# Fourteen of sixteen up projection groups as seven half-block products, and up and down units in alternation, in a one-core decoder layer

## The reference

```python
def channel_mlp(x, g, w_up, w_down):
    h = rmsnorm(x, g)
    u = jnp.maximum(jnp.einsum('btd,df->btf', h, w_up), 0)
    return jnp.einsum('btf,fd->btd', u * u, w_down)
```

## Time and profile before

| | |
|---|---|
| time, median of 3 runs | 2390.11 us (2389.84 to 2390.34) |
| span of the profiled execution | 2388.1 us (that execution's own time is not given apart from its span; the median lies 2.0 us above the span) |
| PE busy | 2362.5 us, 99% of the span |
| DVE busy | 1377.4 us, 58% |
| ACT busy | 963.6 us, 40% |
| DMA | 224.28 MB, 94 GB/s |

### The profile page before, as it was taken

How to read it: one execution, slowest core, us unless ns; L and a number is a source line. 1 busy time by engine, 2 the same in 40 slices (tenths; PEclk the granted TensorE clock), 3 DMA queues, 4 the chain that set the end, 5 groups by cost and what they waited for, 6 DMA issues and landing times.

```text
span 2388.1 us, 33521 instructions
## 1 busy us (share of the span) xinstructions
PE 2362.5 (99%) x13086; PEld 2016.6 (84%) x13086; DVE 1377.4 (58%) x3162; ACT 963.6 (40%) x2050; POOL 79.3 (3%) x136
## 2 busy tenths in 40 slices
PE   9999999999999999999999999999999999999998
PEld 8988888888897888888998788888888879889996
DVE  4478554456378654455456854554656785555555
ACT  4445433334345533334333543333434454333332
POOL 3000000000000000000000210000010000000000
PEclk9999999999999999999999999999999999999999
DMA  6212323333511223324421233223444122222221
GB/s 193 79 45 90 96 97 98 96 109 106 170 55 54 81 96 97 96 90 132 147 80 37 68 99 97 90 96 97 133 124 133 45 67 88 77 84 80 88 80 66
DMA packets 175402, 224.28 MB, mean 94 GB/s; under 512 B 15107, under 2 KB 126308, under 8 KB 175228
## 3 DMA queue, kind: packets, MB, share of 16 engines
q1 hardware_dynamic: 162636, 192.63, 25.8%
q10 hardware_dynamic: 6448, 19.40, 2.3%
q0 software_dynamic: 6160, 10.11, 1.6%
HBM read 210.72 MB, written 12.60 MB: 94 GB/s over the span
## 4 chain that ended last, share of the span: by engine, by line
PE 95%; DVE 4%; ACT 1%; issue 1%; DVEq 0%; ACTq 0%
PE ps L2066 28%; PE ps L2068 28%; PE ps L2067 27%; PE ps L2077 2%; PE ps L2207 2%; PE ps L2187 1%; PE ps L2196 1%; PE ps L2253 1%; PE ps L2256 1%; DVE w_lo L1177 1%; PE ps L2103 0%; PE ps L2596 0%; PE ps L2115 0%; PE ps L2232 0%; DVE w_lo L1173 0%
## 5 line engine op out<-in xcount | busy, mean ns | idle before, releaser
L2068 PE MATMUL ps<-a_hi,w_lo 128*128 128x512 f32 (+2 forms) x1672 | 583.9, 349 | 0.0
L2066 PE MATMUL ps<-a_hi,w_hi 128*128 128x512 f32 (+2 forms) x1672 | 582.1, 348 | 0.6 <-DVE a_lo L1181 0.2
L2067 PE MATMUL ps<-a_lo,w_hi 128*128 128x512 f32 (+2 forms) x1672 | 582.0, 348 | 0.0
L702 ACT ACTIVATE w_hi<-w_raw,gains 128x256 fp32r<-128x256 f32 (+1 forms) x576 | 253.2, 521 | 411.3 <-PE ps L2068 290.6
L2066 PE MATMUL ps<-w_hi,u_all 128*128 128x512 f32 x1024 | 403.8, 394 | 0.0
L2068 PE MATMUL ps<-w_hi,u_all 128*128 128x512 f32 x1024 | 403.8, 394 | 0.0
L2067 PE MATMUL ps<-w_lo,u_all 128*128 128x512 f32 x1024 | 401.3, 392 | 0.0
L2066 PEld LDWEIGHTS ps<-a_hi,w_hi 128*128 128x128 f32 x1672 | 315.8, 189 | 43.1 <-DVE a_lo L1181 1.4
L2067 PEld LDWEIGHTS ps<-a_lo,w_hi 128*128 128x128 f32 x1672 | 314.0, 188 | 40.9
L2068 PEld LDWEIGHTS ps<-a_hi,w_lo 128*128 128x128 f32 x1672 | 314.2, 188 | 39.4
L1181 DVE TENSOR_TENSOR x<-x,ps 128x512 f32<-128x512 f32 (+1 forms) x288 | 196.5, 686 | 259.8 <-PE ps L2068 241.9
(11 more groups left out here) (378 smaller groups left out, 2336.1 us busy)
## 6 DMA issues: line engine op xcount, KB each, us to landing
w_raw<-in_w_up_dram SPq DMA_DIRECT2D x128, 512.0 KB, 3.7
w_raw<-in_w_down_dram SPq DMA_DIRECT2D x128, 512.0 KB, 3.5
w_raw<-in_w_out_dram SPq DMA_DIRECT2D x32, 512.0 KB, 3.5
w_raw<-in_w_in_dram SPq DMA_DIRECT2D x24, 580.0 KB, 4.9
w_raw<-in_w_in_dram SPq DMA_DIRECT2D x22, 512.0 KB, 3.7
w_raw<-in_w_in_dram SPq DMA_DIRECT2D x32, 256.0 KB, 2.9
wide<-in_x_prompt_dram ACTq DMA_DIRECT2D x12, 512.0 KB, 4.6
x<-in_x_prompt_dram ACTq DMA_DIRECT2D x9, 512.0 KB, 6.2
```

Source lines behind the costliest of these rows:

```text
L702: ins = eng.activation(w_hi[b][:, k * n:(k + 1) * n][:, s], src[:, s], ACT.Copy, scale=gain[:, a:a + 1])
L2066: eng.matmul(out, lh, rh, start=(k == ks[0]), stop=False)
L2067: eng.matmul(out, lh, rl, start=False, stop=False)
L2068: ins = eng.matmul(out, ll, rh, start=False, stop=(k == last))
```

## The change

For 14 of the 16 up units of a quarter (all but U(0, 0) and U(0, 1)), the product of a 256 x 1024 block of weights with a 1024 x 512 block of tokens is seen as 2 x 2 blocks, and made with seven half-block products in place of eight, after the scheme of Strassen in Winograd's form. A half-block product is 4 steps of contraction x 3 = 12 matmuls of 256 tokens (320 in products 0, 1, 2 and 6 of the fourth quarter). Around it:

- The norm's gain goes onto the tokens: DVE takes each turned half tile out of PSUM times the gain into `x_all` (`take_tile`, two operations for a tile), and ACT and DVE split from there. Weights of up units are no longer scaled.
- Four sums of token blocks, and their split, are made once in a quarter (`x_sums`, `t_high_part`, `t_low_part`).
- For each such unit DVE makes four sums of weight blocks (`sum_forms`), ACT seven rounded parts (`high_form`), DVE seven rests (`low_form`), each of 512 elements; they lie in a ring of nine slots in what were the two unit buffers.
- The seven results are added up by ACT (`take_copy`) and DVE (`take_sum`, seven steps) into `c_at` in the tile `wide`; ACT then does relu, square and copy in SBUF (`square_up`), DVE the rest (`low_up`).
- Up and down units alternate: U(c, 0), D(c-1, 0), U(c, 1), D(c-1, 1), so that U(7, 1) is unit 42, where it was unit 41.
- Memory: the bias moves into a region that the MLP overwrites and is fetched again by POOL in each quarter; two of the tiles ahead lie in `PT`; the squares of `stats_ahead` are written to a region that holds token sums until all products are done, so it waits for `m_done`.
- In DVE's `step`, the pieces for the next quarter now stand at the end, behind the loop over the down unit's results.

```diff
+MLP_ORDER = [("U", 0, 0), ("U", 0, 1)]
+for _c in range(1, NC):
+    MLP_ORDER += [(kind, _c - (kind == "D"), half) for half in range(2) for kind in "UD"]
+MLP_ORDER += [("D", NC - 1, 0), ("D", NC - 1, 1)]
...
+FORMS_OF = "A11 A12 S1 S2 S4 S3 A22".split()
...
             def stats_ahead(q, b):
 
+                eng.wait_ge(m_done.sem, m_done.at(q, 0))
...
-                    if u == UNITS - 4 and not last:
-                        scale_ahead(q + 1, 0)
-                    if u == UNITS - 3 and not last:
-                        take_ahead(q + 1, 0)
-                    if u == UNITS - 2 and not last:
-                        scale_ahead(q + 1, 1)
-                    if u == UNITS - 1 and not last:
-                        take_ahead(q + 1, 1)
...
+                        eng.wait_ge(dn_read.sem, dn_read.at(q, 2 * NT * c))
+                        next_part(0)
+                        if before is not None:
+                            low_sum(before, 0)
+                        next_part(1)
                         for n, (j, R) in enumerate(down_tiles(last, u)):
...
+                            if n < 3:
+                                next_part(n + 2)
...
+                        next_part(5)
+                    if u == UNITS - 4 and not last:
+                        scale_ahead(q + 1, 0)
+                    if u == UNITS - 3 and not last:
+                        take_ahead(q + 1, 0)
+                    if u == UNITS - 2 and not last:
+                        scale_ahead(q + 1, 1)
+                    if u == UNITS - 1 and not last:
+                        take_ahead(q + 1, 1)
...
+                def product(u, f, w, right):
+
+                    eng.wait_ge(f_split.sem, f_split.at(q, 7 * seven(u) + f + 1))
+                    hi, lo = form_at(w_hi_all, u, f), form_at(w_lo_all, u, f)
+                    out = product_bank(seven(u), f)[:, 0:w]
+                    for k in range(4):
+                        rh, rl = right(k, w)
+                        eng.matmul(out, hi[:, k, :], rh, start=(k == 0), stop=False)
+                        eng.matmul(out, hi[:, k, :], rl, start=False, stop=False)
+                        ins = eng.matmul(out, lo[:, k, :], rh, start=False, stop=(k == 3))
+                    ins.then_inc(m_done.sem, 1)
...
                 def step(u, kind, c, half):
                     if u == UNITS - 3 and not last:
-                        eng.wait_ge(up_read.sem, up_read.at(q + 1, 0))
+                        eng.wait_ge(cp_ok.sem, cp_ok.at(q + 1, 0))
+                        eng.wait_ge(c_add.sem, c_add.at(q + 1, 0))
                         turn_ahead(q + 1, 0)
```

More of the change, by code:

```diff
@@ L56 @@
 WMAX = KT * TMW
+FORM = 512
+T_ALL = 6424
+T_SECOND = 4376
+RING = 9
+N_PLAIN = 2
 def unit_of(u):
@@ L193, in hymba_layer @@
         bgate = sb("bgate", [P, 2 * HM])
+        kk_forms = other("kk_forms", [P, 2, P + TMAX], F32R)
         kk = sb("kk", [P, 2, P + TMAX])
@@ L229, in hymba_layer @@
         oms = sb("oms", [NS, HM, DV], where=phase)
+        bias = sb("bias", [P, H, 2 * P], where=phase)
         phase.close()
@@ L368, in unit_shape @@
             kind, i, w = unit_of(u)
[L369 to L380, removed]
+            return (4, 512) if kind == "O" or kind == "M" and mlp_unit(u)[0] == "D" else (KT, w)
         block = ctx.enter_context(nc.Block())
@@ new lines, in hymba_layer, with staging, x_flat @@
+        HT = TQ // 2
+        def staging(last):
+            T, ws = (TMAX, HT + NS) if last else (TQ, HT)
+            line = flat(wide)
+            c_at = [line[:, i * T:(i + 1) * T] for i in range(2)]
+            at = 2 * T + ws
+            s1, r6, h5, s5 = (line[:, a:b] for a, b in ((2 * T, at), (at, at + HT), (at + HT, at + 2 * HT), (at + 2 * HT, at + 2 * HT + NS)))
+            return ws, c_at, s1, r6, h5, s5
+        def x_flat(last):
+            w = TMAX + NS if last else TMAX
+            starts = (4 * w, 8 * w + (2 * TQ if last else 4 * TMAX))
+            return [x_all[:, at:at + 4 * v].rearrange("p (k t) -> p k t", k=4) for at, v in zip(starts, (w, TMAX))]
@@ L481, in turned_bank, with t_src, product_bank, ahead_tile @@
+        def t_src(last, name):
+            one, two = x_flat(last)
+            end = TMAX if last else TQ
+            return {"T1": one[:, :, HT:end], "T3": one[:, :, 0:HT], "T2": two[:, :, 0:HT], "T4": two[:, :, HT:end]}[name]
+        def product_bank(at, n):
+            return ps[(7 * at + n + 2) % 4]
+        def ahead_tile(j):
+            return PT[:, 2 * j:2 * j + 2, :].rearrange("p a b -> p (a b)") if j < 2 else xn_tile(j)
+        def spare():
+            return t_plain[:, 0:D]
         def turned_bank(q, n):
@@ new lines, in plain_up @@
+                def plain_up(u):
+                    kind, c, half = mlp_unit(u)
+                    for n, (t, s) in enumerate(up_order(u, NN)):
+                        off, w = splits[s]
+                        o = half * 2 * NN + n
+                        eng.wait_ge(up_out.sem, up_out.at(q, o + 1))
+                        if n == 0 and half:
+                            eng.wait_ge(u_split.sem, u_split.at(q, 2 * NN))
+                        elif n == 0 and last:
+                            eng.wait_ge(turned.sem, turned.at(q, 2 * NT))
+                        mine = c_at[t][:, off:off + w]
+                        eng.activation(mine, ps[(o + 2) % 4][:, 0:w], ACT.Relu).then_inc(up_read.sem, 1)
+                        eng.wait_ge(up_read.sem, up_read.at(q, o + 1))
+                        eng.activation(mine, mine, ACT.Square).then_inc(u_sq.sem, 1)
+                        eng.wait_ge(u_sq.sem, u_sq.at(q, o + 1))
+                        eng.activation(u_hi[0][:, half * 2 + t, off:off + w], mine, ACT.Copy).then_inc(u_high.sem, 1)
@@ L1988, in step @@
-                            eng.wait_ge(u_sq.sem, u_sq.at(q, o + 1))
-                            low(l, o, t, off, w)
-                            if n == NN - 1 and not end and u != U_M:
-                                split_vec(eng, nq, nu, 1, i)
+                            low_up(u, t, off, w, half * 2 * NN + n + 1)
+                        if half:
+                            for n in (3, 4, 5):
+                                next_part(n)
+                        else:
+                            t_low_part(2)
```

694 lines of the change are left out of this document (505 added, 189 removed).

## The result

| kernel | median us (lowest to highest) | profiled execution's span |
|---|---|---|
| before | 2390.23 (2389.84 to 2390.92, 4 runs) | 2388.1 |
| changed | 2403.95 (2402.36 to 2404.09, 4 runs) | 2402.2 |

The changed kernel takes 1.0056 times as long (95% interval 1.0042 to 1.007). It is slower by 0.56%, where 2382 us and a faster kernel were forecast, and it lies 1 us above the range.

A forecast was written before the change was run, and what follows sets the result against it. PE, busy 99% of the span, was taken as the bound, so time is matmuls plus PE's new waits. 64.6 us saved less 56.3 of waits gave 8.3 us, a 2382 us median; range 2358 to 2403 us (8 in 10).

The forecast's parts named there:

- What a changed unit saves: Up units on PE: 11.12 to 10.01 us in three quarters, 12.56 to 11.26 in the fourth; together 64.6 us saved.
- the second rival: 256-column matmuls on PE run at 0.1133 us instead of 0.1192; all at that pace gives 2358 us; chance 0.22.
- DVE in the steady run: Alternating MLP units: DVE's 10.5 us list fits a down unit's 11.12 us, so new vector and scalar work costs nothing.
- The thin cover: Rival in the changed units: products wait 0.2 us each, 2393 us, or 0.4 us, 2404 us; chance 0.08.
- 1, ahead of the MLP: Before the MLP, four times: PE waits for later takes, copies and rests of tiles, 2.5 us each, total 10.0.
- 2, first changed unit: First seven-product unit, four times: products 2 and 5 come late by 0.3 and 0.9 us, total 4.8.
- 3, U(7, 1) to D(6, 1): Between these units, three times: PE's transposes wait for last addition, squares and scaling, 5.7 us each, total 17.1.
- 4, ahead of D(7, 1): Before this down unit, three times: second `scale_ahead` waits for D(7, 0)'s last result, 2.95 us each, total 8.9.
- 5, next quarter: Start of next quarter, three times: `take_ahead` begins only when the last result is read, 5.15 us each, total 15.5.
- the sum: Whole program: 64.6 us saved less 56.3 of PE waits is 8.3 us, median 2382 us; given 0.40.
- The cold start: PE restarts at half pace behind its waits, 2.5 us each: 2397 us for six waits, 2404 with D(7, 1)'s; chance 0.28.
- the first rival: PE starts cold again behind its waits at quarter ends, 2.5 us each, making the kernel slower, 2397 or 2404 us; chance 0.28.

The follow-up runs named there:

- Experiment 5: Tiles moved in SBUF; in the changed kernel the weight ring shifted 64 bytes: 2392.98 us, 128 bytes: 2394.51, 32 bytes: 2405.90; weights and activations together 64 bytes: 2404.25 us.
- experiment 3: The kernel before with its last `take_ahead` (next quarter's second tile) moved behind the loop of the last down unit: 2411.98 us, 21.8 us more.
- e7_before_pad: The kernel before with 64 bytes left free between the weights and the activations in SBUF: 2393.43 us in one run, 2.5 us more.

## Why the prediction was wrong

**What a changed unit saves: right.** 84 x 0.1192 = 10.01 us was forecast and 9.97 measured, 11.26 and 11.29 in quarter 4. 42 x 1.15 + 14 x 1.27 = 66.1 us against the 64.6 of the forecast. The faster pace that the second rival asked for did not come by itself; it took a shift of 64 bytes, and then for four of seven products.

**DVE in the steady run: right.** No wait of PE there. The thin cover did not show.

**The five places: each there, the sizes close.** In us, over the whole program; places 1 and 2 from the timelines of both kernels, the clock from the starts of matmuls:

| place | forecast | measured | clock behind it |
|---|---|---|---|
| 1, ahead of the MLP | 10.0 | 13.5 (3.1, 3.1, 3.3 and 4.0) | 1.6, in quarter 4 |
| 2, first changed unit | 4.8 | 4.6 (11.50 - 9.97 = 1.53 in three quarters, none in the fourth) | none |
| 3, U(7, 1) to D(6, 1) | 17.1 | 17.3 | 7.2 |
| 4, ahead of D(7, 1) | 8.9 | 8.0 | 6.2 |
| 5, next quarter | 15.5 | 14.7 | 7 |

The waits make 58.1 us against 56.3. That error and the one in the saving all but cancel.

**The step that failed is the sum, which priced the waits by their length alone.** The cold start was worked out as a rival, 2.5 us each, and given 0.28. It was set aside because "the waits are short, and weight loads or transposes may fall into them". The windows show 0.46 us of PE's work and 0.03 of weight loads in 5 us: all that PE had left to do stood behind the wait, in program order, and that could be read from the order beforehand. The rival's own number with place 4, 2404 us, is what was measured: 9 x 2.5 = 22.5 us against 20.4 us at these nine waits, and 1.6 at a tenth. Its size was in part luck: 2.5 us came from the program's start, where the granted clock read 1.00, and the single prices are 1.7 to 3.0. What the first rival took from the Trainium skill ("TensorE: Matmul & The Clock Gate", HAM oscillation) is what these rows show, at waits of 2.67 us too. The sum as it should have stood: 2382 - 1.5 + 1.8 + 22 = 2404 us against 2403.95.

**The chances.** The argument against the rival was a guess, the one for it came from rows 9, so it should have had the larger chance. The range ended at 2403, 1 us below the rival's own 2404, for no reason that the text gives.

**The range's other end**, the faster pace, rested on a row that had been read rightly (the alternation is real) without its cause. Experiment 5 gives its size here: some 10 us, by a move that the change did not make.

## What to carry to other kernels

When PE is the bound and a change gives it new waits, price each as its length plus a restart at half clock, unless the order shows work of PE in the wait. Here that was 1.4 to 2.8 us behind every wait of 4.9 us or more, and 1.5 to 3.0 us behind about half of those of 2 to 2.7 us. The row to look at is the granted clock in a window over the wait, not the list of waits. An operation moved from ahead of a loop to behind it can cost more than the arithmetic saved: one such move in the kernel before cost 22 us, and putting two of them back in the changed one gave 33. Where no work can be found for the wait, multiplications whose result nobody reads kept the clock up and gave 16 us. And where waits of 2 us stand, a difference of some us between two kernels can be the clock: count the stretches at half clock in both traces before it is put down to the edit.

## What the runs showed of the hardware

- Whether a short wait loses the clock differs from one execution to the next. In the traces of the ten kernels with seven products and of experiment 3, counted over all waits of PE of one length (the price is what the matmuls behind it took longer than at full clock):

| wait of PE, us | place | lost the clock | price, us |
|---|---|---|---|
| 5.65 to 6.05 | 3 | 18 of 18 | 1.4 to 2.8 |
| 4.9 | 5 | 18 of 18 | 1.5 to 2.7 |
| 2.67 | 4 | 11 of 18 | 1.5 to 3.0 |
| 2.0 to 2.1 | 1 | 21 of 40 | 1.5 to 1.7 |

A window behind place 4 of the changed kernel, where the clock fell, and one over its wait at place 1 in quarter 1, where it did not:

```profile
572.00:576.00 4.00, 4.00 (x20) 3.87 (x21) 1.60 (x2) 3.11 (x13) 0.00 (x0) 0.62 0.30 78
```

```profile
232.50:234.50 2.00, 0.05 (x1) 0.00 (x0) 1.88 (x3) 1.98 (x3) 0.00 (x0) 1.00 0.00 0
```

- The clock also fell without a wait. In eight of the thirteen executions, not in those of the two kernels compared here, it did so once in quarter 4 behind some 5 us of matmuls of 129 and 32 columns (the mLSTM), at 1.5 to 3.4 us. Windows over and behind such a row in the trace of the kernel before with its activations moved (e7_before_pad):

```profile
1770.00:1775.50 5.50, 5.44 (x89) 4.54 (x88) 2.93 (x10) 1.75 (x3) 0.00 (x0) 1.00 0.57 134
1775.50:1782.00 6.50, 6.50 (x28) 5.10 (x29) 1.34 (x5) 0.00 (x0) 1.23 (x2) 0.50 0.44 108
```

- The pace of a 256-column matmul, 0.113 or 0.119 us, goes with the distance in SBUF between its two tiles: moving both by 64 bytes changed nothing, moving one by 64 took up to 5% off four of seven products. The down units' 48 matmuls of 512 took 11.09 us with the ring at 0 or 64 bytes, 11.06 at 128 and 11.21 at 32, 1% that 64 such units turn into 7.7 us. Which distances are fast in general is open.
